# Fourteen down-projection phases as seven half-sized block products, with the operand sums on GpSimd

## The reference, cut to what matters

```python
# first block, layers i = 0, 1:  D = 1024, D_FF = 4096
u = jnp.square(jax.nn.relu(h @ mlp_w1[i])) @ mlp_w2[i]
h = _layer_norm(DN_ALPHA * h + u, ln2_g[i], ln2_b[i])
# second block, layers 0, 1: two such layers each, D_FF_2 = 2816
x = x + 0.5 * (jax.nn.silu(h @ w_gate) * (h @ w_up)) @ w_down
```

## Time and profile before

| | |
|---|---|
| runs | 3756.57, 3758.97, 3764.41 us (median 3758.97) |
| profiled execution, span | 3762.2 us |
| PE busy | 3680.7 us (98%) |
| PE in the chain that ended last | 85% |
| DVE busy | 1884.2 us (50%) |
| ACT busy | 1433.2 us (38%) |
| POOL busy | 152.6 us (4%) |

### The profile page before, as it was taken

The page is one execution under the profiler, slowest core; times in us unless marked ns, Lnnn a source line. Parts: engine busy times, 40 slices in busy tenths (PEclk is TensorE's granted clock), DMA queues, the critical chain, the costliest instruction groups (busy, mean ns, idle before and its releaser), DMA issues.

```text
span 3762.2 us, 46018 instructions
## 1 busy us (share of the span) xinstructions
PE 3680.7 (98%) x18208; PEld 3004.4 (80%) x18208; DVE 1884.2 (50%) x2668; ACT 1433.2 (38%) x2168; POOL 152.6 (4%) x149
## 2 busy tenths in 40 slices
PE   9999899999999999999999999999999999999999
PEld 7776788887678888888877898888888877888887
DVE  4455644366754445433367564334433476564333
ACT  3345332336534223332255443323332354443322
POOL 0001000000100000000000310000000000310000
PEclk9999999999999999999999999999999999999999
DMA  4000222222013223222221012222322221012221
GB/s 180 34 34 34 79 91 100 93 98 93 21 53 116 90 101 110 92 101 95 90 92 48 12 63 101 90 101 84 112 91 100 73 103 48 18 57 101 101 91 72
DMA packets 45285, 306.91 MB, mean 82 GB/s; under 512 B 5136, under 2 KB 5520, under 8 KB 10640
## 3 DMA queue, kind: packets, MB, share of 16 engines
q1 hardware_dynamic: 45072, 303.97, 22.9%
HBM read 301.86 MB, written 2.10 MB: 81 GB/s over the span
## 4 chain that ended last, share of the span: by engine, by line
PE 85%; DVE 9%; ACT 4%; issue 1%; DMA 0%; DVEq 0%; POOL 0%; ACTq 0%; SPq 0%; POOLq 0%
PE ps L445 83%; ACT arena L1159 2%; PE ps L454 2%; DVE split L2092 2%; DVE arena L2096 2%; DVE arena L2092 2%; DVE X L2096 1%; ACT split L1159 1%; DVE arena L2943 1%; ACT L1159 0%; DVE arena L2088 0%; DVE small L2108 0%; DVE arena L2120 0%; DVE arena L2100 0%; DMA X<-in_x 0%
## 5 line engine op out<-in xcount | busy, mean ns | idle before, releaser
L445 PE MATMUL ps<-split 128*128 128x512 f32 (+2 forms) x13596 | 3086.5, 386 | 23.5 <-DVE X L2096 7.0
L445 PEld LDWEIGHTS ps<-split 128*128 128x128 f32 x13596 | 2479.1, 189 | 551.1 <-issue 48.8
L2092 DVE TENSOR_TENSOR split<-ring,split 128x1024 fp32r<-128x1024 f32 x554 | 676.1, 1220 | 1185.7 <-ACT split L1159 1168.2
L1159 ACT ACTIVATE split<-ring 128x1024 fp32r<-128x1024 f32 x554 | 582.8, 1052 | 1247.2 <-PE ps L445 1207.0
L445 PE MATMUL ps<-arena 128*128 128x128 f32 (+9 forms) x3344 | 487.1, 298 | 24.9 <-DVE arena L2092 9.7
L445 PEld LDWEIGHTS ps<-arena 128*128 128x128 f32 (+2 forms) x3344 | 395.6, 191 | 100.1 <-issue 68.7
L1159 ACT ACTIVATE arena<-ps 128x512 f32<-128x512 f32 (+6 forms) x580 | 298.0, 514 | 383.3 <-PE ps L445 217.9
L2092 DVE TENSOR_TENSOR arena<-arena 128x512 f32<-128x512 f32 (+5 forms) x254 | 150.6, 593 | 69.5 <-ACT split L1159 49.8
L1159 ACT ACTIVATE split<-arena 128x512 fp32r<-128x512 f32 x156 | 98.7, 633 | 165.3 <-DVE arena L2092 163.1
L2092 DVE TENSOR_TENSOR arena<-arena,ps 128x512 f32<-128x512 f32 x176 | 121.0, 688 | 41.3 <-PE ps L445 21.5
L2092 DVE TENSOR_TENSOR split<-arena,split 128x512 fp32r<-128x512 f32 x156 | 108.0, 692 | 64.2 <-ACT split L1159 61.6
(11 more groups left out here) (99 smaller groups left out, 968.7 us busy)
## 6 DMA issues: line engine op xcount, KB each, us to landing
ring<-in_wts SPq DMA_DIRECT2D x268, 1024.0 KB, 4.8
ring<-in_wts SPq DMA_DIRECT2D x25, 512.0 KB, 3.4
X<-in_x SPq DMA_DIRECT2D x4, 512.0 KB, 6.0
out<-arena SPq DMA_DIRECT2D x4, 512.0 KB, 2.6
ring<-in_wts SPq DMA_DIRECT2D x2, 784.0 KB, 5.6
C<-in_cb SPq DMA_DIRECT2D x1, 1403.5 KB, 14.5
ring<-in_wts SPq DMA_DIRECT2D x2, 576.0 KB, 10.5
C<-in_cb SPq DMA_DIRECT2D x1, 512.0 KB, 6.4
```

The costliest lines, as they stand in the source:

```text
L445: return e.matmul(out, l, r, start=start, stop=stop, skip_group_check=True)
L1159: o.sig(a.activation(out, i, f, **kw), sig)
L2092: o.sig(v.tensor_tensor(out, a, b, op), sig)
```

## The change

In 14 phases (MLP phases 0, 1, 2 of two layers; phases 0 and 1 of the four layers of the second block) the down projection becomes a `unit`. With the activations cut into quarters a11, a12, a21, a22 (first index: 256 positions; second: 4 of the 8 k-tiles) and the weights into b11, b12, b21, b22 (4 k-tiles x 512 columns, one ring slot each), it computes seven products of quarter size instead of eight:

```diff
+PRODUCTS = (("P1", "b11", "a11"), ("N5", "t1", "f5"), ("P6", "t2", "f6"), ("N3", "b22", "f3"),
+            ("P7", "t3", "f7"), ("P2", "b21", "a12"), ("N4", "t4", "a22"))
```

GpSimd makes the four summed activation quarters and the four summed weight blocks (the latter in halves of 128x1024, some in place in the ring):

```diff
+        g.wait_ge(S[f"free{last.i}"], last.n + 1)
+        for x, (f, a, b, op) in enumerate(((1, "a21", "a22", ALU.subtract), (2, "sum", "a11", ALU.subtract),
+                                           (3, "sum", "a12", ALU.add), (4, "a11", "a21", ALU.subtract))):
...
+            if x in (1, 2):
+                g.wait_ge(S["form"], f.i)
+            g.tensor_tensor(M.source(f), M.quarter(f, a), M.quarter(f, b), op).then_inc(S["shape"], 1)
+        for x, (what, q, ld, until) in enumerate(U.sums):
...
+            g.wait_ge(S[f"ring{ld.slot}"], ld.landed)
+            if until:
+                g.wait_ge(S["lo"], until)
+            if x > 1:
+                g.wait_ge(S["sum"], U.first + x - 2)
+            out, one, two = {"t1": (t14, r["b11"], r["b12"]), "t2": (r["b11"], t14, r["b22"]),
+                             "t3": (r["b12"], r["b12"], r["b22"]), "t4": (t14, r["b11"], r["b21"])}[what]
+            g.tensor_tensor(out, one, two, ALU.add).then_inc(S["sum"], 1)
```

The activations of a phase are now kept unsplit in `M.raw`: on DVE the MLP does one operation per bank (`max` and `mult` with relu's output) instead of two. Each of the seven left factors is split once (`form`: ACT copies hi, DVE subtracts for lo, 128x1024). The first four forms of a unit stand beside the last column groups of the `up` ahead of it, the other three inside the unit (here the vector program's):

```diff
+    def unit(name, alpha, s, then=()):
...
+        prime(name)
+        for r in range(7):
+            for q in range(2):
+                if r == 0 or q == 0:
+                    next(side, None)
+                    next(side, None)
+                for p in ps[2 * r + 2 + q:2 * r + 3 + q]:
+                    split(p)
...
+            if 1 <= r <= 3:
+                form(fs[r + 3])
+            elif r >= 4:
+                next(then, None)
```

In the MLP (first line) the four forms come one after each piece of the last column group; in the second block (second line) they are spaced two pieces apart, over two column groups, starting with the second one:

```diff
+            up(p + 1, formed(lins[f"dn{l}{p}"].forms[0:4]))
...
+            up(p + 1, spaced(formed(lins[f"fd{w}{l}{p}"].forms[0:4])))
```

The last phase of each layer stays as two `lin`, reading four formed quarters. A ring slot is now also held until the sums that read it are done:

```diff
+            if loads[ld.i - NS].added:
+                s.wait_ge(S["sum"], loads[ld.i - NS].added)
```

More of the change, by code:

```diff
@@ L211, in plan @@
 def plan():
-    lins, loads, turned, n = {}, [], [], 0
+    lins, loads, turned, forms, n = {}, [], [], [], 0
+    sums, shapes = 0, 0
     def load(name, key, k0, nk, c0, ncol):
@@ L266, in mlp @@
                     between=[(f"pt{l}", f"pT_{l}", 0, 2, 0, 512)] if p + c == 4 else ())
+            lins[f"dn{l}{p}0"].forms = quarters
+            for pc in lins[f"dn{l}{p}1"].pieces[-3:]:
+                pc.form = quarters[3].i + 1
+            for f in quarters:
+                f.end = n
         load(f"ln2{l}", f"ln2_{l}", 0, 1, 0, 2048)
@@ L295, in ffn @@
                 lin(f"fd{n_}{l}{p}{c}", f"fd{n_}_{l}", TILES[p], c * 512, 512, False, kbase=8 * p, between=[row] if p + c == 3 else ())
+            lins[f"fd{n_}{l}{p}0"].forms = quarters
+            for pc in lins[f"fd{n_}{l}{p}1"].pieces[-3:]:
+                pc.form = quarters[3].i + 1
+            for f in quarters:
+                f.end = n
     for l in range(2):
@@ L768, in up @@
                     lin(f"up{l}{p}{c}", H)
-            ucount += 8
         up(0)
@@ L1176, in prime, with lin @@
             split(p)
-    def lin(name, evict=None, primed=False, mix=None, then=None, ms=range(4)):
+    def lin(name, evict=None, primed=False, mix=None, then=None, ms=range(4), beside=none):
         nonlocal side
@@ L1197, in lin @@
                     split(ahead[q])
+                next(beside, None)
                 continue
@@ L1546, in mlp_ple @@
         up(0)
-        for p in range(4):
-            if p < 3:
-                up(p + 1)
-            for c in range(2):
-                lin(f"dn{l}{p}{c}", embedded() if p + c == 3 and p == 3 else idle())
+        for p in range(3):
+            up(p + 1, formed(lins[f"dn{l}{p}"].forms[0:4]))
+            more = unit(f"dn{l}{p}", lins[f"dn{l}30"].forms if p == 2 else ())
+        lin(f"dn{l}30", embedded(), beside=more)
+        lin(f"dn{l}31", idle())
         name = f"lx2{l}"
@@ new lines, in unit @@
+    def unit(name, alpha, s, then=()):
+        nonlocal side
+        ps, fs, then, more = lins[name].pieces, lins[name].forms, formed(then), added(name, alpha, s)
+        prime(name)
+        for r in range(7):
+            for q in range(2):
+                if r == 0 or q == 0:
+                    next(side, None)
+                    next(side, None)
+                for p in ps[2 * r + 2 + q:2 * r + 3 + q]:
+                    split(p)
+            if r == 0:
+                flush()
+                side = more
+            if 1 <= r <= 3:
+                form(fs[r + 3])
+            elif r >= 4:
+                next(then, None)
+        return then
@@ L3221, in pool_program @@
         pass
+    for p in range(3):
+        unit(f"dn0{p}")
     O = K.o
@@ L3253, in pool_program @@
             rotation(3)
+    for p in range(3):
+        unit(f"dn1{p}")
     r0, r1 = K.SM[:, 24:28], K.SM[:, 20:24]
@@ L3260, in pool_program @@
     for l in range(2):
+        for p in range(2):
+            unit(f"fd1{l}{p}")
         g.wait_ge(*K.turn[f"hx{l}", 3, 1].full)
@@ L3297, in pool_program @@
             lower(t)
+        for p in range(2):
+            unit(f"fd2{l}{p}")
 def sync_program(s, K, S, W, loads):
```

358 lines of the change are left out of this document (264 added, 94 removed).

## The result

| | before | changed |
|---|---|---|
| median of 4 runs | 3761.69 us | 3787.09 us |
| range | 3756.57 to 3764.94 | 3783.28 to 3789.14 |
| profiled span | 3762.2 us | 3786.1 us |

The ratio is 1.0064, with a 95% interval of 1.005 to 1.0078. The time lies within the range of the prediction (3710 to 3790), 3 us from its upper end. But the forecast case was "no change" (3758), the chances leaned to faster (0.43, against 0.32 for slower), and the kernel became slower.

What follows compares the result with a forecast made beforehand. TensorE was taken to bound the kernel, busy 98% of the span. Removing matmuls saves 76.2 us, but late splits leave -4.2 us, plus 3 for the clock: -1 in total, 3758 us on the median, range 3710 to 3790.

Steps and rivals of the forecast that it cites:

- The collision: In the units, VectorE's two-SBUF-input splits and forms alternate with GpSimd's additions, one turn taking 3.29 us.
- An MLP unit ... +4.5 us: MLP unit followed by another: nine turns make N3 late by 8.6 us, P7 1.4 more; 48.1 us against 43.5.
- The third unit of a layer ... +2.5: Last MLP unit of a layer: no successor's sum, so one addition less (2.0 us); +2.5 us.
- A round with a form is 1.48 + 3 x 1.33 = 5.47 us: VectorE, second to fourth round of a unit: it keeps pace with TensorE's 5.44 us but cannot make up delay.
- The six last additions ... and the forms of its last phase ... nothing: Layer's end on VectorE: additions (4.4 us) and forms fit its 14 us free in the following `lin`; cost nothing.
- A unit of the second block ... -2.9 us: Second block, four units: sums start earlier, N3's split is late 2.5 us, unit 40.6 us; -2.9 us each.
- The clock step: MLP units: TensorE's wait before N3 drops the clock to 0.50; 3 us for four units together, bounds 0 and 12.
- The second unit of a layer ... -3.9: Second block, four units: no successor, starts about 0.9 us later, N3 late 1.5 us; -3.9 us each.
- The port is held for the whole instruction: Slower rival for VectorE beside GpSimd in the units: a turn is 3.6 us; +26, 3785 us; chance 0.12.
- The clock falls in each wait: Slower rival for the six MLP units: 3 us and more in each; +18, 3777 us; chance 0.10.
- Shorter additions: Faster rival for GpSimd: additions of 2.1 us, a turn 3.05, or less waiting; -22 or more, 3730 us; chance 0.20.
- no collision: Faster rival for the units: additions run before VectorE needs the port; -76, 3683 us; chance 0.08.

Runs made afterwards that it cites:

- e1: Changed kernel with all twelve GpSimd additions of a unit cut from 1024 to 64 columns, sums not computed in full: 3687.4 us, ratio 0.9801.
- e2: Changed kernel with each GpSimd addition replaced by writes of about the same length, sums zero: 3685.8 us, ratio 0.98.
- e3: Changed kernel with twelve unread matmuls put ahead of N3 in every unit, so TensorE doesn't stand still: 3780.93 us, ratio 1.0052.
- e4: Changed kernel with the first four forms of each MLP unit a column group earlier, so sums can start earlier: 3751.13 us, ratio 0.9976.
- e6: e4 with weight sum t3 computed before t2: 3733.13 us, ratio 0.993.
- e7: e6 with the three forms inside a unit one round later and the next unit's first activation sum held until form f7: 3716.01 us, ratio 0.9884.
- e10: e7 with the six last additions of a layer moved on VectorE behind the last form: 3706.3 us, ratio 0.9856.
- e12: e7 with VectorE's last-phase forms cut to 256 columns (192 in the second block), not computed in full: 3699.81 us, ratio 0.9838.

## Why the prediction failed

**Right.** The gain: 76.2 us said, 73.5 measured in e1. The collision, its kind and its place: e1 and e2 show that it takes the whole gain back and more, and evictions with one SBUF operand stay at 1.49 for two. The order of events in an MLP unit, with the long wait before N3; up phases at full pace; ring loads still at 4.8 us.

**Wrong by its size**, about 25 us in all (+23.9 us from span to span where -1 was said), and so no "no change" either. These terms of the sum failed:

1. *"An MLP unit ... +4.5 us"*: measured +5.9, from the distance of 92.9 us between units (an up phase of 43.5 and a unit of 49.4 us). An addition takes 2.40 us, not 2.34, and a turn 3.36, not 3.29; nine turns put N3's second split at 28.3, not 27.6. P7 follows at 32.7, not 31.7. Four units x 1.4 = 5 to 6 us.
2. *"The third unit of a layer ... +2.5"*: the layer's rest after two units at 5.9 is +4.4 and +5.6, so 2 to 3 us more each, 5 us together. The addition less did what was said on VectorE: N3's second split ends at 731.21, 2.0 us sooner than a unit's distance behind the one at 640.34. But TensorE starts N3 at the same place (729.99, 92.9 behind 637.08), and it isn't in front at the layer's end, because it runs at a granted clock of 0.50 at first and then meets a full VectorE. That is the step on VectorE's own work: *"A round with a form is 1.48 + 3 x 1.33 = 5.47 us"* left out one gap of 0.10, and *"The six last additions ... and the forms of its last phase ... nothing"* was true only for a VectorE that is on time. VectorE in that unit in the changed kernel, N3's splits and then what stands behind them:

```profile
728.28 2.93 DVE L2248 TENSOR_TENSOR split<-ring,split 128x1024 fp32r<-128x1024 f32 x2
...
735.72 1.23 DVE L2248 TENSOR_TENSOR split<-ring,split 128x1024 fp32r<-128x1024 f32 x1 [0.25 <-ACT split L1283]
737.05 1.23 DVE L2248 TENSOR_TENSOR split<-arena,split 128x1024 fp32r<-128x1024 f32 x1
738.38 1.49 DVE L2252 SCALAR_TENSOR_TENSOR X<-ps,X 128x512 f32<-128x512 f32 x2
739.97 2.56 DVE L2248 TENSOR_TENSOR split<-ring,split 128x1024 fp32r<-128x1024 f32 x2
742.63 1.23 DVE L2248 TENSOR_TENSOR split<-arena,split 128x1024 fp32r<-128x1024 f32 x1
```

   From form to form it is 742.63 - 737.05 = 5.58 us without a gap, against TensorE's 5.44, and the rounds with last-phase forms come on top of the three counted. Nothing is caught up until the layer's end; e3 shows it as the 1.14 us wait.
3. *"A unit of the second block ... -2.9 us"*, four times: measured about -0.6 in the first layer (the ACT copies at the start of this unit and of the next stand at 1735.70 and 1843.93; the 108.2 us between them less three column groups of 21.76 leave 42.9, where 43.5 stood before). The wait was 3.03 us, not 2.5, and the clock was at 0.50 behind it:

```profile
1760.45 102.88 PE L535 MATMUL ps<-split 128*128 128x512 f32 x444 [3.03 <-DVE split L2248]
1863.62 3.02 PE L535 MATMUL ps<-split 128*128 128x512 f32 x12 [0.29 <-DVE split L2248]
1867.91 22.56 PE L535 MATMUL ps<-split 128*128 128x512 f32 x96 [1.28 <-issue]
1891.08 9.17 PE L535 MATMUL ps<-split 128*128 128x512 f32 x39 [0.61 <-DVE split L2248]
```

   The clock step was put to the MLP units alone (3 us in all). e3 shows it costing about 1 us there and about 5 us in the second block. Together 9 us.
4. *"The second unit of a layer ... -3.9"*, four times: measured about -1.6, from the layer's mean of -2.2. Its waits are the last three of these rows: 2.2 us in sum, more than the 1.5 said. They stand ahead of N3, at N3 and 23 us behind it, where only N3 was reckoned with, and the last is in a round with last-phase forms. Another 9 us.
5. *"TensorE's other matmuls stay."* The mixers are at +1.1 each. In one of them TensorE's twelve matmuls at 2040 us take 4.59 us, at a granted clock of 0.50 from 2042 to 2044; the same twelve took 3.02 before. It isn't the collisions: e1, which has none, has +1.0 in the second mixer. Why the clock falls there wasn't tried.

1 to 4 come to 28 or 29 us of loss, less the 3 us charged for the clock; the mixers (+2.2) and the start (-2.9) nearly cancel.

**The rivals.** *The port is held for the whole instruction* gave 3785, next to the 3787 measured, but that is chance: by the full length of both a turn would be 2.40 + 1.23 = 3.63 us, the rival was to decide from 3.4 us on, and the rows show 3.36. The rule of the Trainium skill ("SBUF — State Buffer", section "Who interferes with whom") is right in its direction; for the length of a turn the measurement decides. *The clock falls in each wait* holds for the clock itself, but most of its price was hidden: with the clock held up e3 gains 6 us, not 18. *Shorter additions* and *no collision* fell: an addition takes 2.40, and e2 shows the collision.

The first step has a turn a little too short. The other three have one fault in common: each unit was reckoned up to the first late split and then taken to be back in step. With VectorE at 5.58 us for TensorE's 5.44, lateness stays and adds to whatever comes next. The sum was also thin: 76 us of gain against 75 of cost, so that a third more of cost (100 us) turned "no change" into 25 us slower although the collision had been seen.

## What to carry to other kernels

Before work is moved to GpSimd, count the VectorE instructions with two SBUF inputs that stand beside it, and give each pair one turn (here 3.36 us), not the longer of the two. Then look at when the additions run, rather than at how many there are: the same twelve cost 100 us where they met the splits that TensorE waited for, and each step that drew them and VectorE's splits and forms apart gave 17 to 36 us (e4, e6, e7), though the long wait was still there after e6; with e10 the whole change turned from +25 to -55 us. And where an engine needs as long for a round as the one it feeds, later work on it stops being free once it is late (e10, e12), even work that costs nothing when it is on time (e1).

## What was not expected of the hardware

A row of twelve matmuls between two waits lasts 2.98 to 3.06 us, where twelve in an unbroken stream take 2.72. That isn't a slower pace: rows of 24 last 5.72 (e7) and rows of 264 last 60.23 to 60.27 (59.85 at 0.2267 us each), so 0.3 to 0.4 us are added once per row, however long it is (a single matmul lasts 0.39 us, though in a stream the next starts 0.227 behind it). A wait of 0.3 us in such a row is therefore about 0.6 us by which the next matmul starts late (617.00 - 613.70 = 3.30, less 2.72). GpSimd's writes (1.98 us for two of 128x1024) went beside VectorE's two-input subtractions without stretching one (1.232 us in the mean, as before). And a stretch at half the clock, 24 matmuls in 7.32 us rather than 5.72, cost nothing where the next split was late anyway, and about 1.2 us of its 1.6 where it wasn't.
